# Seven instead of six seven-product chunks in each half of a float32 decoder block's last projection

## The reference

```python
hf = rmsnorm(x, norm_ffn[l])
act = jax.nn.silu(hf @ w_gate[l]) * (hf @ w_up[l])      # 256 x 5632
x = x + act @ w_down[l]                                  # 5632 x 2048
return rmsnorm(x, norm_final)
```

## Time and profile before

| | us |
|---|---|
| median of 3 runs | 1692.24 (1692.17 to 1692.29) |
| the profiled execution's own time | 1693.11 |
| its span, first to last instruction | 1691.3 |
| PE busy in the span | 1675.6 (99%) |
| DVE busy | 1445.7 (85%) |
| ACT busy | 918.5 (54%) |
| POOL busy | 71.0 (4%) |

### The profile page before, as it was taken

The page is one execution under the profiler, slowest core; times in us unless marked ns, Lnnn a source line. Parts: engine busy times, 40 slices in busy tenths (PEclk is TensorE's granted clock), DMA queues, the critical chain, the costliest instruction groups (busy, mean ns, idle before and its releaser), DMA issues.

```text
span 1691.3 us, 19896 instructions
## 1 busy us (share of the span) xinstructions
PE 1675.6 (99%) x7521; PEld 1385.2 (82%) x7521; DVE 1445.7 (85%) x1272; ACT 918.5 (54%) x795; POOL 71.0 (4%) x66
## 2 busy tenths in 40 slices
PE   9999999999999999999999999999999999999997
PEld 7888888888888888888888877888888888888886
DVE  6988557698898998888987499999999999898987
ACT  6655444455545555555544455565656555655554
POOL 1000111300000000000000010000000000230000
PEclk9999999999999999999999999999999999999999
DMA  9465555556566655555556556556666666566653
GB/s 376 155 219 199 174 183 184 185 189 235 199 216 230 220 199 199 200 198 199 197 182 219 185 166 220 201 198 198 198 198 198 199 199 201 195 201 222 222 192 108
DMA packets 124496, 340.88 MB, mean 202 GB/s; under 512 B 7436, under 2 KB 7564, under 8 KB 123784
## 3 DMA queue, kind: packets, MB, share of 16 engines
q1 hardware_dynamic: 122592, 334.68, 58.8%
q10 hardware_dynamic: 1832, 5.22, 1.0%
HBM read 333.60 MB, written 2.10 MB: 198 GB/s over the span
## 4 chain that ended last, share of the span: by engine, by line
PE 88%; DVE 7%; issue 2%; DMA 1%; ACTq 1%; ACT 1%; POOL 0%; DVEq 0%; POOLq 0%; SPq 0%
PE ps L1946 11%; PE ps L1953 11%; PE ps L1947 11%; PE ps L2249 8%; PE ps L2255 8%; PE ps L2251 8%; PE ps L2330 4%; PE ps L2331 4%; PE ps L2335 4%; PE ps L1874 4%; PE ps L1875 4%; PE ps L1883 4%; DVE w_lo L1135 2%; PE ps L1974 1%; PE ps L1975 1%
## 5 line engine op out<-in xcount | busy, mean ns | idle before, releaser
L1135 DVE TENSOR_TENSOR w_lo<-w_raw,w_hi 128x2048 fp32r<-128x2048 f32 x307 | 706.4, 2304 | 72.7 <-ACT w_hi L654 71.2
L654 ACT ACTIVATE w_hi<-w_raw 128x2048 fp32r<-128x2048 f32 (+1 forms) x311 | 588.3, 1896 | 331.6 <-issue 119.3
L1946 PE MATMUL ps<-w_hi,xT_hi 128*128 128x512 f32 x570 | 222.6, 391 | 0.4 <-DVE cb L1303 0.3
L1947 PE MATMUL ps<-w_hi,xT_lo 128*128 128x512 f32 x570 | 222.0, 390 | 0.0
L654 ACT ACTIVATE t_hi<-t_raw 128x1536 fp32r<-128x1536 f32 x56 | 83.3, 1488 | 127.4 <-PE ps L2255 87.1
L1953 PE MATMUL ps<-w_lo,xT_hi 128*128 128x512 f32 x570 | 150.6, 390 | 0.3 <-DVE w_lo L1135 0.3
L2249 PE MATMUL ps<-w_hi,fT_hi 128*128 128x512 f32 x352 | 139.4, 396 | 2.9 <-ACT w_hi L654 1.8
L2251 PE MATMUL ps<-w_hi,fT_lo 128*128 128x512 f32 x352 | 137.4, 390 | 0.0
L1946 PEld LDWEIGHTS ps<-w_hi,xT_hi 128*128 128x128 f32 x570 | 107.1, 188 | 23.3 <-DVE cb L1303 1.2
L1953 PEld LDWEIGHTS ps<-w_lo,xT_hi 128*128 128x128 f32 x570 | 106.8, 188 | 23.6 <-DVE w_lo L1135 1.6
L1947 PEld LDWEIGHTS ps<-w_hi,xT_lo 128*128 128x128 f32 x570 | 107.1, 188 | 22.0
(11 more groups left out here) (441 smaller groups left out, 3104.5 us busy)
## 6 DMA issues: line engine op xcount, KB each, us to landing
w_raw<-in_w_in SPq DMA_DIRECT2D x126, 1024.0 KB, 4.9
w_raw<-in_w_gate SPq DMA_DIRECT2D x88, 512.0 KB, 3.8
w_raw<-in_w_up SPq DMA_DIRECT2D x88, 512.0 KB, 4.6
w_raw<-in_w_down SPq DMA_DIRECT2D x44, 1024.0 KB, 5.1
w_raw<-in_w_branch_b SPq DMA_DIRECT2D x16, 1024.0 KB, 5.2
w_raw<-in_w_branch_a SPq DMA_DIRECT2D x16, 1024.0 KB, 5.1
w_raw<-in_w_out SPq DMA_DIRECT2D x16, 1024.0 KB, 5.7
late<-nat ACTq DMA_DIRECT2D x6, 448.0 KB
```

The source lines that it names most:

```text
L654: copy = lambda o, i, **kw: nc.scalar.activation(o, i, ACT.Copy, **kw)
L1135: V.tensor_tensor(w_lo[:, chunk.split, :], w_raw[:, chunk.raw, :], w_hi[:, chunk.split, :].bitcast(F32), ALU.subtract).then_inc(lo_split, 1)
L1946: T.matmul(ps[:, banks[name], :], tile(0, t), moving(0, u), start=begins, stop=False)
L1947: last = T.matmul(ps[:, banks[name], :], tile(1, t), moving(0, u), start=False, stop=False)
```

## The change

Place 18 stays the last and 3 the first seven-product chunk of each half; 9, 12 and 15 make room for 8, 11, 13 and 16. There are then seven of them in each half, at distances of 3, 2, 3, 2, 3 and 2 chunks, instead of six at distances of 3. The forms of each of the seven have a tensor of their own; the seventh lies behind the raw forms, since the old place holds six.

```diff
-DOWN_S = (3, 6, 9, 12, 15, 18)
+DOWN_S = (3, 6, 8, 11, 13, 16, 18)
...
-        down_form_hi = at("down_form_hi", [P, 4 * ND, P], F32R, LATE_F + 4096)
-        down_form_lo = at("down_form_lo", [P, 4 * ND, P], F32R, LATE_F + AT + 4096)
+        down_form_hi, down_form_lo = ([at(f"down_form_{n}{d}", [P, 4, P], F32R, LATE_F + h * AT + 4096 + 2048 * d if d < 6
+                                          else R1 + 4096 + 2048 * h) for d in range(ND)]
+                                      for h, n in enumerate(["hi", "lo"]))
         down_form_raw = at("down_form_raw", [P, 2, 4, P], F32, R1)
-        assert 4 * ND * P * 4 <= AT - 4096
+        assert ND <= 7
...
-                        copy(down_form_hi[:, 4 * d:4 * d + 4, :], down_form_raw[:, d % 2]).then_inc(
+                        copy(down_form_hi[d][:], down_form_raw[:, d % 2]).then_inc(
...
-                        V.tensor_tensor(down_form_lo[:, 4 * d:4 * d + 4, :], down_form_raw[:, d % 2],
-                                        down_form_hi[:, 4 * d:4 * d + 4, :].bitcast(F32),
+                        V.tensor_tensor(down_form_lo[d][:], down_form_raw[:, d % 2], down_form_hi[d][:].bitcast(F32),
                                         ALU.subtract).then_inc(down_form_lo_done, 1)
...
-                    n = 4 * DOWN_S.index(c % DN) + ("D1", "S1", "S2", "S4").index(name)
-                    return (down_form_hi, down_form_lo)[part][:, n, :]
+                    form = (down_form_hi, down_form_lo)[part][DOWN_S.index(c % DN)]
+                    return form[:, ("D1", "S1", "S2", "S4").index(name), :]
```

## The result

| | before | changed |
|---|---|---|
| median (runs) | 1692.38 us (8) | 1697.18 us (8) |
| lowest to highest | 1692.17 to 1693.03 | 1696.77 to 1697.72 |
| profiled execution | 1693.11 | 1697.22 |
| span | 1691.3 | 1695.2 |

The ratio is 1.0028, 95% interval 1.0018 to 1.0037: slower by 4.8 us, with six matmuls fewer. The forecast was 1697.6.

A forecast was written before the change was run, and what follows sets the result against it. PE, busy 1675.6 of 1691.3 us, was taken as the bound, with DVE hardly ahead in the first half. First half +5.1 and second +0.2 gave +5.3 us: median 1697.6, range 1696 to 1699.5, chance 0.68.

The forecast's parts named there:

- Matmuls, 1.36 us saved: One more chunk per half goes from 24 to 21 matmuls: 0.68 us a half saved if PE never waits.
- Chunk 7 2.02 us late, 12 the same, 17 0.95: First half: the sums, with 0.51 us from POOL, stand ahead of a_lo on DVE, so PE starts these chunks late.
- The 0.22 us that PE needs a DVE result ahead: Latency from a DVE result's end to PE's matmul, read at chunk 3; leaves 0.13 us spare at chunk 6.
- Each ends where a POOL row ends: Three DVE instructions beside POOL's forms in the first half, lengthened by 1.06 us, end at or just behind POOL rows.
- 0.39 at the low part of chunk 8 and of 13: First half: t_hi waits for the sums, so w_lo comes 0.39 us late for PE's low part.
- Second half, 0.25 a pair and 0.16 behind the gain, +0.2: The one t_hi buffer costs 0.75 us over three pairs, a_lo behind chunk 40's gain multiplication 0.16; 0.68 saved.
- What decides is the order within it: A distance-two pair needs 11.5 us of DVE against 10.2 of PE, cannot hide itself; the order within it decides.
- Edits at nothing: The sums' transfer, the seventh down_form_hi (0.6 us, in ACT's idle time) and the new addresses cost nothing.
- A: Rival, chance 0.09: DVE's lead at chunks 6, 11 and 16 covers the sums; 1690.9 to 1691.8 us.
- B: Rival, chance 0.13: sums don't meet POOL's forms, first pairs cost 1.2 us, the third none; 1693.5 to 1695.3.
- C: Rival, chance 0.07: delay passed on, POOL costs the sums up to 1.06, first-half pairs 3 us each; 1700 to 1701.
- D: Rival, chance 0.03: the new waits drop PE's clock to 1.2 GHz for a chunk; 1703 for one, 1708 for two.

The follow-up runs named there:

- e5: Changed kernel with two buffers for t_hi and t_lo used in turn: second half 114.83 us, projection 236.12, median 1696.86 us, ratio 1.0028 against the kernel before.
- e3: Changed kernel with the sums for a close pair's second chunk behind a_lo of the chunk between on DVE: projection 238.85, median 1698.88 us, ratio 1.0034.
- e7: Changed kernel with a_hi of seven-product chunks copied ahead of t_hi and w_hi on ACT: projection 231.84, median 1692.15 us, ratio 1.0000.
- e1: Changed kernel with the six old places 3, 6, 9, 12, 15, 18 and the forms' new tensors: projection 232.06, median 1692.77 us, ratio 0.9999.
- e2: Changed kernel with six seven-product chunks in each half, unevenly at 3, 6, 8, 11, 13, 18: projection 236.66, median 1696.97 us, ratio 1.0025.
- e9: Changed kernel with a_hi ahead of t_hi and w_hi, POOL's forms started earlier, and two t_hi/t_lo buffers: projection 230.93, median 1691.30 us, ratio 0.9994.
- e4: Changed kernel with POOL's forms, from the third set on, started in DVE's idle time: projection 234.55, median 1695.43 us, ratio 1.0015.

## Why the prediction was right, and where its reasons were not

- *Matmuls, 1.36 us saved*: right. e5's second half shows 0.70 for its half with all waits gone.
- *Chunk 7 2.02 us late, 12 the same, 17 0.95*: came 1.83, 1.90 and 0.95 with the wider spacing of the matmul behind it, each for `a_lo`, as named. POOL took 0.42 from the sums instead of 0.51, and PE took up `a_lo` 0.14 us behind its end, not 0.22. The Trainium skill's rule of exclusion ("SBUF — State Buffer", "Who interferes with whom") agrees: the sums were held up by these 0.42 us, which no row of before could show.
- *The 0.22 us that PE needs a DVE result ahead*: read from the wrong place. PE did not wait at chunk 3. Its first low matmul, at 1470.50, is 3.17 us behind the chunk's first matmul, just as at chunk 6, where the prediction itself finds time to spare. The row of that first one:

```profile
1467.33 0.39 PE L2330 MATMUL ps<-w_hi,a_hi 128*128 128x512 f32 x1
```

So 0.22 was an upper bound. Where PE waited in the changed kernel, its matmul starts 0.14 to 0.15 us behind the end of `a_lo` and 0.05 behind that of `w_lo`, and the next matmul is 0.07 and 0.11 later than usual: 0.21 and 0.16 in all. That the 0.22 served is luck.

- *"Each ends where a POOL row ends"*: the rows do not show that. The three DVE instructions end at 1485.81, 1486.68 and 1489.14. POOL's rows end 0.69, 0.40 and 0.39 us behind the *starts* of these instructions. The price of 1.06 comes from the durations and stands.
- *0.39 at the low part of chunk 8 and of 13*: came 0.3, since PE took up `w_lo` sooner than the 0.22 put in (above). First half: +4.79 for +5.1.
- *Second half, 0.25 a pair and 0.16 behind the gain, +0.2*: came 0.23 to 0.25 a pair and 0.23 behind the gain, counted to the end of the chunks that wait, +0.28; released by PE as said, and e5 takes all of it away. In the first half `t_hi` of chunks 8 and 13 was released by the sums, as said.
- *"What decides is the order within it"*: right only in part. Order matters: e3 moved the sums and lost 1.8 us more, e7 moved one copy on ACT and took the loss back. What the runs refute is that the loss lies in `a_lo` standing behind the sums on DVE. It lies in DVE's whole cycle with its idle time, 28.1 us against 25.84. I had put 11.5 us to a pair and left out the 1.07 that DVE stands in front of `a_lo`. The measured cycle is 12.18: that 11.5, plus 1.07 and 0.1 at the ends of the gap, less the 0.51 of POOL's that falls behind the end of this cycle, on the next sums. The sum did not suffer, since it was built from start times and not from the 11.5, and the 3.85 from `t_hi` to `a_lo` in the `t_hi` step contained the idle time. But the cheapest remedy, e7, could not be seen from the text as it stood.
- *Edits at nothing*: right (e1).
- *Rivals*: A did not come, for the lead was not there. B did not: the sums met POOL's forms, and the third pair cost 0.95. C did not: the sums bore 0.42 and not 1.06, the second pair cost what the first did, and in the second half PE did not wait for `a_lo` of 31 and 36. D is excluded by the granted clock, 1.00.

The sum of +5.3 was 0.2 us over the trace's +5.07. The median moved by 4.80, within the scatter that the time ahead of the projection brings.

## What to carry to other kernels

An engine that is 99% busy can still depend on a helper whose cycle has 0.1 us to spare: read the helper's cycle from start to start, idle time included, and compare that with the main engine's, for the new spacing, before counting saved instructions. As long as that helper has no time to spare, even spacing can be worth more than one item more: two pairs at distance two in each half cost 4.6 us (e2), where a seventh chunk saves 0.68 a half; with DVE's idle time and half of POOL's interference out of the way (e9) all but 0.25 of the 1.36 us comes in at the same uneven places. And where a helper stands still in a full cycle, look at the order in the queue of the engine that it waits for: a copy that was ready to be made stood behind two that were needed later.

## What the hardware showed that I had not expected

POOL's three instructions for one set of forms cost DVE between next to nothing (e4 at chunk 8, where DVE stands still for 1.81 us) and 1.1 us (a full queue), by nothing but the moment at which they begin. In the changed kernel's full queue three of DVE's next instructions are longer, `w_lo` by 0.55 and two sums by 0.27 and 0.15, and no row shows idle time or names POOL as the releaser. In e7 at chunk 6, where `t_lo` started about 0.09 us behind the end of `down_form_lo`, POOL's first instruction (0.75 us) started together with `t_lo`, and `t_lo`, elsewhere 1.75, took 2.35.
